# Modulation vectors summed as rows in column quarters, front norms with factors by tokens

## The chip, the cores and the metric

The kernel runs on one core of a Trainium2 chip. The metric is the device time of one execution in microseconds (us), lower is better. Matrix products run on TensorE (PE in the profile; its weight loads are PEld), elementwise work on VectorE (DVE) and ScalarE (ACT), and GpSimd (POOL) and SyncE (SP) mostly issue transfers. All matrix results land in PSUM, eight banks of 128 partitions x 512 values of four bytes; everything else on the chip lies in SBUF.

## The reference

Two transformer-like blocks run one after the other on x, 512 tokens x 1024 features. The first block has two layers (a recurrent mixer, then forgetting attention), each with an MLP of width 4096. The second block has two layers with a linear-attention mixer and a gated MLP, and each of its layers is modulated by six vectors that come from one conditioning vector c:

```python
c_act = jax.nn.silu(c)
for l in range(DEPTH):
    mod = c_act @ ada_w[l] + ada_b[l]              # (1, 6144)
    sh1, sc1, gt1, sh2, sc2, gt2 = [m[:, None, :] for m in jnp.split(mod, 6, axis=-1)]
    h = rms_norm_2(x, norm1_g[l]) * (1 + sc1) + sh1
    p = h @ w_in[l]                                # with v_down beside it in layer 1
    ...
    x = x + gt1 * (mixed @ w_out[l])
    h2 = rms_norm_2(x, norm2_g[l]) * (1 + sc2) + sh2
    gate, up = jnp.split(h2 @ w_gu[l], 2, axis=-1)
    x = x + gt2 * ((jax.nn.silu(gate) * up) @ w_down[l])
```

`rms_norm_2` divides each token by the root of the mean of its 1024 squares plus 1e-6. The change is about `mod` and about the norm in front of `w_in` in both layers.

## The kernel before, in words

x is kept transposed: eight tiles `xT[:, t, :]` of 128 features x 512 tokens. Every weight matrix comes in slabs of 1024 rows x 256 columns. SP fetches a slab into `raw`; ACT rounds it to a high part `whi` (function `hi`, line 848) and DVE makes the low part `wlo = raw - whi` (function `lo`, line 1522). PE then makes three products a tile: high x high, high x low, low x high (lines 2386 to 2388 with the weights stationary, 2445 to 2447 with 128 tokens stationary and 256 weight columns moving). `raw`, `whi` and `wlo` hold two slabs each. A slab costs PE about 11 us, ACT 1.9 us and DVE 2.3 us. The products of small tables in plain four-byte floats show as two records each, every one with its own weight load.

The order of work on each engine is written out by hand. Class `Plan` numbers all products that take a PSUM bank; job j uses bank j mod 8, and PE waits in `start` until job j - 8 was read (`ahead` waits the same way without starting the job). `evacuated` waits until a bank was read, `ready` until it was written. SP's order of slabs is the order in which PE uses them.

**The modulation.** While the first block's MLPs run (`mlp1`, layer 0 for the first vectors, layer 1 for the second), POOL fetches `ada_w` and DVE multiplies and adds it into `ada_acc`, 128 partitions x 6144 columns: the sum over the eight groups of 128 rows, so that only the sum over the partitions is left. `adaln` on PE makes this last sum with 48 products: a block of 128 columns of `ada_acc` stationary, a single column of ones moving, so that each gives one column of 128 values, which is the layout that the rest needs. `adaln` on DVE then adds the bias and makes `gmod`, `shc`. For layer 0 these 48 products stand beside the matmuls of slab "v 0" of the attention layer (`adaln_beside`, line 2605, two products in each of the 24 steps of token blocks 1 to 3, the last one behind them, line 2609); their result is read by DVE after the key heads of slab "k 0". For layer 1 they stand in one piece (line 2484) at the front of the second block.

**The front norm of the second block.** For norms 4 (layer 0) and 6 (layer 1), ACT squares the tiles of x (`norm_squares`, line 878), DVE adds the eight squares (`norm_sums`, lines 1533 and 1536), and PE multiplies by a full matrix of 1/1024 (`mean_square`, line 2467), so that all 128 partitions hold the mean of each of 512 tokens. ACT takes the root of 128 x 512 values (`norm_root`, line 883), DVE the reciprocal (line 1541), and then tile by tile DVE makes value = x * gain * factor (line 1555), ACT the high part (line 890), DVE the low part (line 1562). The first projection, slab "lat", starts with the tile that is ready (`before=normed`), then "gl1" and "k2" follow. Norm 4's squares start only after the last addition to x of the first block (line 1664, add x and the product of the last `down` slab); norm 6's squares already stand between the last additions of layer 0 of the second block.

Steps that the prediction compares with: the head means (line 2477, `head_means`), the token-wise mean of norm 2 (line 2594, four products), the factor rows of norm 0 (line 2537, four products of a broadcast column with the identity), the head factors (line 2797, 32 products with 64 stationary columns and 128 moving), the state inputs (line 2859, 48 products of 64 x 64 x 64) and the pool products (line 3108, four of 512 columns). Line 1666 is DVE's addition to x that reads PSUM with a scale.

## Time and profile before

| | |
|---|---|
| Median of 3 runs | 2925.84 us (2925.13 to 2927.65) |
| Profiled execution, span | 2918.1 us |
| PE busy | 2791.1 us |
| DVE busy | 1587.6 us |
| ACT busy | 988.9 us |
| Bytes read from memory | 277.09 MB |

The span is the time from the first to the last instruction of one profiled execution; the measured time of a run has some us around it. Starts are in us from the start of the span. "PEclk" is the clock that TensorE was granted, 1.00 for 2.4 GHz and 0.50 for 1.2 GHz.

### The profile page before, as it was taken

What the parts mean: (1) busy time and instruction counts of PE and PEld (TensorE: products, weight loads), DVE (VectorE), ACT (ScalarE), POOL (GpSimd) and SP (SyncE); (2) the same over time, 40 slices, a digit from 0 to 9 for tenths busy, and PEclk for the clock granted to TensorE, in tenths of its full rate; (3) what the DMA queues carried; (4) which work ended last, traced back from release to release, by engine and by line L of the source; (5) the groups of instructions that cost most, each with busy time, mean ns of one, the idle gap of its engine ahead of it and who ended that gap; (6) DMA issues with size and microseconds to landing.
All of it is one profiled execution on the core that took longest, in us unless ns stands there. A gap on an engine that the chain in (4) does not pass through costs nothing.

```text
span 2918.1 us, 46007 instructions
## 1 busy us (share of the span) xinstructions
PE 2791.1 (96%) x19577; PEld 2317.3 (79%) x19577; DVE 1587.6 (54%) x2309; ACT 988.9 (34%) x1354; POOL 200.0 (7%) x251
## 2 busy tenths in 40 slices
PE   8899999999999999998899999999988999999998
PEld 7778888897788888777878788887667778888887
DVE  5658777854677777465443553334575443543334
ACT  5643222335532212333333332223533333332223
POOL 4100000000000000010040000000020030000000
PEclk9999999999999999799999999999889999999999
DMA  4334555421145554210022322322220013223222
GB/s 150 101 104 131 180 165 173 156 64 53 52 130 177 176 168 152 66 58 12 3 77 89 99 90 98 101 97 72 72 64 6 24 52 101 95 93 101 95 93 72
DMA packets 238532, 281.98 MB, mean 97 GB/s; under 512 B 7444, under 2 KB 224856, under 8 KB 238344
## 3 DMA queue, kind: packets, MB, share of 16 engines
q1 hardware_dynamic: 225312, 227.07, 24.3%
q0 software_dynamic: 12896, 52.11, 6.0%
q8 instruction: 150, 2.46, 0.4%
q14 instruction: 38, 0.31, 0.0%
q10 hardware_dynamic: 136, 0.03, 0.0%
HBM read 277.09 MB, written 2.10 MB: 96 GB/s over the span
## 4 chain that ended last, share of the span: by engine, by line
PE 91%; DVE 4%; ACT 3%; issue 2%; DMA 0%; ACTq 0%; DVEq 0%; POOL 0%; POOLq 0%
PE psum L2386 25%; PE psum L2388 25%; PE psum L2387 25%; PE psum L2445 1%; PE psum L2446 1%; PE psum L2447 1%; PE psum L2887 1%; PE psum L2902 1%; DVE wlo L1522 1%; PE psum L2484 1%; PE psum L2870 1%; PE psum L2797 1%; ACT whi L848 1%; PE psum L2821 1%; PE psum L2835 1%
## 5 line engine op out<-in xcount | busy, mean ns | idle before, releaser
L2386 PE MATMUL psum<-hh,whi 128*128 128x512 f32 (+1 forms) x2040 | 794.4, 389 | 19.5 <-DVE hl L1562 6.6
L1522 DVE TENSOR_TENSOR wlo<-raw,whi 128x2048 fp32r<-128x2048 f32 x222 | 517.3, 2330 | 514.7 <-ACT whi L848 514.1
L2387 PE MATMUL psum<-hl,whi 128*128 128x512 f32 (+1 forms) x2040 | 787.6, 386 | 0.0
L2388 PE MATMUL psum<-hh,wlo 128*128 128x512 f32 (+1 forms) x2040 | 786.9, 386 | 0.0
L848 ACT ACTIVATE whi<-raw 128x2048 fp32r<-128x2048 f32 x222 | 423.8, 1909 | 550.7 <-PE psum L2388 550.7
L2386 PE MATMUL psum<-mh,whi 128*128 128x512 f32 (+1 forms) x1248 | 486.3, 390 | 3.1 <-issue 2.3
L2387 PE MATMUL psum<-ml,whi 128*128 128x512 f32 (+1 forms) x1248 | 480.1, 385 | 0.0
L2388 PE MATMUL psum<-mh,wlo 128*128 128x512 f32 (+1 forms) x1248 | 479.8, 384 | 0.0
L2386 PEld LDWEIGHTS psum<-hh,whi 128*128 128x128 f32 x2040 | 388.1, 190 | 104.0 <-issue 25.2
L2388 PEld LDWEIGHTS psum<-hh,wlo 128*128 128x128 f32 x2040 | 387.8, 190 | 76.9
L2387 PEld LDWEIGHTS psum<-hl,whi 128*128 128x128 f32 x2040 | 388.0, 190 | 75.9 <-issue 1.0
L2386 PEld LDWEIGHTS psum<-mh,whi 128*128 128x128 f32 x1248 | 235.7, 189 | 48.3 <-issue 4.5
L2388 PEld LDWEIGHTS psum<-mh,wlo 128*128 128x128 f32 x1248 | 235.5, 189 | 46.5
L2387 PEld LDWEIGHTS psum<-ml,whi 128*128 128x128 f32 x1248 | 235.7, 189 | 44.3 <-issue 0.5
L1959 DVE SCALAR_TENSOR_TENSOR rest<-rest,cact 128x192 f32<-128x192 f32 (+1 forms) x448 | 187.7, 419 | 15.8
L1666 DVE SCALAR_TENSOR_TENSOR xT<-psum,mod,xT 128x512 f32<-128x512 f32 x64 | 47.4, 750 | 156.2 <-PE psum L2388 156.2
L1201 ACT ACTIVATE mh<-rest 128x512 fp32r<-128x512 f32 x64 | 40.5, 633 | 253.0 <-DVE rest L1970 253.0
L788 POOL DMA_DIRECT2D rest<-in_ada_w x64 | 56.7, 887 | 920.0 <-DVE rest L1959 618.8
L1664 DVE TENSOR_TENSOR xT<-xT,psum 128x512 f32<-128x512 f32 x80 | 54.5, 684 | 108.7 <-PE psum L2388 108.7
L2333 DVE TENSOR_TENSOR rest<-rest,psum 128x512 f32<-128x512 f32 x40 | 27.5, 688 | 110.8 <-PE psum L2388 110.8
L1480 ACT ACTIVATE mh<-rest 128x512 fp32r<-128x512 f32 x44 | 27.8, 633 | 174.3 <-DVE rest L2333 172.8
L1473 ACT ACTIVATE rest<-psum 128x512 f32<-128x512 f32 x40 | 23.9, 598 | 143.4 <-PE psum L2388 143.2
(451 smaller groups left out, 2848.0 us busy)
## 6 DMA issues: line engine op xcount, KB each, us to landing
rest<-in_ada_w POOLq DMA_DIRECT2D x64, 768.0 KB, 5.3
raw<-in_w_gu SPq DMA_DIRECT2D x44, 1024.0 KB, 5.1
raw<-in_w_in SPq DMA_DIRECT2D x34, 1024.0 KB, 5.2
raw<-in_w_mlp_in SPq DMA_DIRECT2D x32, 1024.0 KB, 5.4
raw<-in_w_mlp_out SPq DMA_DIRECT2D x32, 1024.0 KB, 5.1
raw<-in_w_out SPq DMA_DIRECT2D x16, 1024.0 KB, 5.1
raw<-in_w_down SPq DMA_DIRECT2D x16, 1024.0 KB, 5.1
raw<-in_w_mem_kv SPq DMA_DIRECT2D x8, 1024.0 KB, 5.2
```

Source lines behind the costliest of these rows:

```text
L788: pool.dma_start(ada[:, s % 2, :, :], w[:, :, bass.ds(c * (per * ADA_COLS) + s * ADA_COLS, ADA_COLS)])\
L848: act.activation(whi[:, g % 2, :, :], raw[:, g % 2, :, :], ACT.Copy).then_inc(hi_done, 1)
L1201: act.activation(mh[:, m, :], f_t[:, m % 2, :], ACT.Square).then_inc(hid_hi, 1)
L1522: ins = dve.tensor_tensor(wlo[:, g % 2, :, :], raw[:, g % 2, :, :], f32(whi[:, g % 2, :, :]), ALU.subtract)
L1664: free(dve.tensor_tensor(xT[:, t, :], xT[:, t, :], bank(j), ALU.add), j)
L1666: free(dve.scalar_tensor_tensor(xT[:, t, :], bank(j), gate, xT[:, t, :], ALU.mult, ALU.add), j)
L1959: ins = dve.scalar_tensor_tensor(acc, w, cact[:, k:k + 1], acc, ALU.mult, ALU.add)
L2386: pe.matmul(out, whi_, xhi, start=first, stop=False)
L2387: pe.matmul(out, whi_, xlo, start=False, stop=False)
L2388: return pe.matmul(out, wlo_, xhi, start=False, stop=last)
L2445: pe.matmul(p[:, 0:n], xh[:, k, t], wh, start=(k == 0), stop=False)
L2446: pe.matmul(p[:, 0:n], xl[:, k, t], wh, start=False, stop=False)
```

## The change

- The last sum over partitions of the modulation is made in rows: 12 products with 32 copies of the ones column stationary and 512 columns of `ada_acc` moving. Four of them fill one bank, each its own quarter of 32 partitions (`modulation_rows`). ACT copies each of the three banks to `ada_rows` (`modulation_row`), and PE turns them with 12 products: a block of 128 columns of the rows stationary, four columns of the identity moving (`modulation_turned`), which give columns i, i+4, i+8, i+12 of 16.
- For layer 0 the rows stand behind slab "v 0", the turning products behind slab "k 0". For layer 1 the rows stand ahead of norm 4's mean, four turning products behind that mean, and eight behind the factor rows.
- Norms 4 and 6: the mean is made by tokens (four products of one column), the root and the reciprocal of 128 x 4 values, then four products spread the factors over the partitions into a bank (`factor_rows`), from which DVE's norm reads directly; the bank is given back at the end of the norm.
- Norm 4's squares and sums stand between the last additions of the first block's MLP, as norm 2's do in layer 0.
- ACT takes a root of `rtok` in place early in the last slabs of the second block's MLPs; its values are not used again.

```diff
--- before.py
+++ after.py
@@ -175,8 +175,10 @@
                 self.slab_jobs("v", 1, 1, NT)
                 self.add("ms", 2)
                 self.slab_jobs("v", 1, 0, NT)
+                for r in range(3):
+                    self.add("mr", 0, r)
+                self.slab_jobs("k", 1, 0, NT)
                 self.add("mod", 0)
-                self.slab_jobs("k", 1, 0, NT)
                 for i in range(4):
                     self.add("hn", 1, i)
                 self.slab_jobs("k", 1, 1, NT)
@@ -199,7 +201,10 @@
                         self.add("ms", 2 * l + 1)
                 self.lin("down", (l, c), 4)
         for l in range(2):
+            for r in range(3) if l == 0 else ():
+                self.add("mr", 1, r)
             self.add("ms", 4 + 2 * l)
+            self.add("rb", 4 + 2 * l)
             if l == 0:
                 self.add("mod", 1)
             self.lin("lat", l, 1)
@@ -446,6 +451,7 @@
         f_v = carve(rest, B + 2 * T, 2, T)
         ada = carve(rest, B + 9 * T, 2, KT, ADA_COLS)
         ada_acc = carve(rest, B + 9 * T + 2 * KT * ADA_COLS, N_MOD)
+        ada_rows = [carve(mo, 2 * B, 3, T), carve(rest, B + 9 * T, 3, T)]
 
         mK = [carve(rest, B, 4, MEM), carve(rest, 0, 4, MEM)]
         mV = [carve(rest, B + 2 * T, MT_, T), carve(rest, 2 * T, MT_, T)]
@@ -877,6 +883,18 @@
                         act.wait_ge(S("norm_added"), 7 * (ni - 1) + max(1, t - 3))
                     act.activation(n_sq[:, t % 3, :], xT[:, t, :], ACT.Square).then_inc(S("norm_sq"), 1)
 
+            def modulation_row(l, r):
+
+                j = J["mr", l, r]
+                ready(act, j)
+                free(act.activation(ada_rows[l][:, r, :], bank(j), ACT.Copy), j)
+
+            def root_tokens(ni):
+
+                j = J["ms", ni]
+                ready(act, j)
+                free(act.activation(tk[:, 0, :], bank(j)[:, 0:NT], ACT.Sqrt, bias=epst[:, 0:1]), j)
+
             def norm_root(ni):
                 j = J["ms", ni]
                 ready(act, j)
@@ -1103,6 +1121,8 @@
                         j = J["v", l, 0, b]
                         ready(act, j)
                         free(act.activation(vtok[:, b, 0:SLAB], bank(j)[:, 0:SLAB], ACT.Copy, scale=tk[:, 1, b:b + 1]), j)
+                    for r in range(3):
+                        modulation_row(0, r)
                     hi(slab_of("k", 1))
                     for i in range(4):
                         evacuated(act, J["memk", 1, i // 2, i % 2])
@@ -1192,7 +1212,8 @@
                             hi(g0 + i + 1)
                             if l == 0 and i >= 5:
                                 raw_hi(2, lambda t: V("norm_mix", 8 + t), (2 * i - 10, 2 * i - 9))
-                                norm_squares(2, (2 * i - 10, 2 * i - 9))
+                            if i >= 5:
+                                norm_squares(2 + 2 * l, (2 * i - 10, 2 * i - 9))
                         else:
                             hi(g0 + i + 1, c, 8, J["up", (l, cc), 0, 0] + 2 * i - 1, 16)
                         for b in range(2) if i < 4 else ():
@@ -1205,12 +1226,14 @@
                 mlp1(CHUNKS1 - 1, 0)
                 if l == 0:
                     raw_hi(2, lambda t: V("norm_mix", 8 + t), (6, 7))
-                    norm_squares(2, (6, 7))
+                norm_squares(2 + 2 * l, (6, 7))
 
             for l in range(2):
                 if l == 0:
-                    norm_squares(4)
-                norm_root(4 + 2 * l)
+                    modulation_row(1, 0)
+                root_tokens(4 + 2 * l)
+                for r in (1, 2) if l == 0 else ():
+                    modulation_row(1, r)
                 norm_hi(4 + 2 * l, (l, 0))
 
                 def own_part(name, s, b, c, dst, rows=P):
@@ -1484,6 +1507,8 @@
                         gated(c, i)
                     for i in range(4):
                         hi(plan.slab["fd", (l, c), i] + 1)
+                        if c == 2 and i == 0:
+                            act.activation(rtok[:, 1, :], rtok[:, 1, :], ACT.Sqrt)
                         if c == 2 and i:
                             norm_squares(6 + 2 * l, (2 * i - 2, 2 * i - 1))
                             if l:
@@ -1535,16 +1560,17 @@
                         dve.wait_ge(S("norm_added"), 7 * (ni - 1) + t - 1)
                         dve.tensor_tensor(n_acc, n_acc, n_sq[:, t % 3, :], ALU.add).then_inc(S("norm_added"), 1)
 
-            def norm(ni, gain, shift=None, slab=None):
+            def norm(ni, gain, shift=None):
 
                 evacuated(dve, J["ms", ni])
-                q.mark(dve.reciprocal(n_rstd, n_rs))
-                if slab is not None:
-                    lo(slab)
-                q.settle()
-                norm_apply(ni, gain, shift)
-
-            def norm_apply(ni, gain, shift=None, between=None):
+                dve.reciprocal(tk[:, 1, :], tk[:, 0, :]).then_inc(S("front_factor"), 1)
+                j = J["rb", ni]
+                ready(dve, j)
+                norm_apply(ni, gain, shift, factor=bank(j))
+                dve.wait_ge(S("norm_lo"), 8 * ni + KT)
+                dve.sem_inc(bank_read[j % BANKS], 1)
+
+            def norm_apply(ni, gain, shift=None, between=None, factor=n_rstd):
 
                 for t in range(KT + 1):
                     if between:
@@ -1552,7 +1578,7 @@
                     if t < KT:
                         if 3 <= t:
                             dve.wait_ge(S("norm_lo"), 8 * ni + t - 2)
-                        dve.scalar_tensor_tensor(n_val[:, t % 3, :], xT[:, t, :], gain(t), n_rstd, ALU.mult, ALU.mult)\
+                        dve.scalar_tensor_tensor(n_val[:, t % 3, :], xT[:, t, :], gain(t), factor, ALU.mult, ALU.mult)\
                            .then_inc(S("norm_val"), 1)
                     if t >= 1:
                         s = t - 1
@@ -1979,20 +2005,19 @@
                                 j, t = J["down", (l, cc), i - 4, b], 2 * (i - 4) + b
                                 ready(dve, j, 16 * c)
                                 add_x(j, t)
-                        if l == 0 and cc == CHUNKS1 - 1 and i >= 5:
-                            raw_lo(2, lambda t: V("norm_mix", 8 + t), (2 * i - 10, 2 * i - 9))
-                            norm_sums(2, range(max(1, 2 * i - 10), 2 * i - 8))
+                        if cc == CHUNKS1 - 1 and i >= 5:
+                            if l == 0:
+                                raw_lo(2, lambda t: V("norm_mix", 8 + t), (2 * i - 10, 2 * i - 9))
+                            norm_sums(2 + 2 * l, range(max(1, 2 * i - 10), 2 * i - 8))
                 mlp1(0, 0)
                 for c in loop(dve, CHUNKS1 - 2):
                     mlp1(1, c)
                 mlp1(CHUNKS1 - 1, 0)
                 if l == 0:
                     raw_lo(2, lambda t: V("norm_mix", 8 + t), (6, 7))
-                    norm_sums(2, (6, 7))
+                norm_sums(2 + 2 * l, (6, 7))
 
             for l in range(2):
-                if l == 0:
-                    norm_sums(4)
                 norm(4 + 2 * l, lambda t: gmod[:, 2 * l, t:t + 1], (l, 0))
                 if l == 0:
                     adaln(1)
@@ -2476,12 +2501,39 @@
                     p = start("hn", l, first + i)
                     done(pe.matmul(p[:, 0:n], m[:, :], sq[:, i, 0:n], start=True, stop=True))
 
-            def adaln(l):
-
-                p = start("mod", l)
+            def modulation_rows(l):
+
                 pe.wait_ge(ada_done, 256 * (l + 1) + 16)
-                for n in range(48):
-                    ins = pe.matmul(p[:, n:n + 1], ada_acc[:, n * P:(n + 1) * P], ones[:, 0:1], start=True, stop=True)
+                for r in range(3):
+                    p = start("mr", l, r)
+                    for c in range(4):
+                        ins = pe.matmul(p[32 * c:32 * c + 32, :], ones[:, 0:1].to_broadcast([P, 32]),
+                                        ada_acc[:, (4 * r + c) * T:(4 * r + c + 1) * T], start=True, stop=True)
+                    done(ins)
+
+            def modulation_turned(l, r, p):
+
+                evacuated(pe, J["mr", l, r])
+                for i in range(4):
+                    ins = pe.matmul(p[:, 16 * r + i:16 * r + 16:4], ada_rows[l][:, r, i * P:(i + 1) * P], ident[:, 0:P:32],
+                                    start=True, stop=True)
+                return ins
+
+            def mean_square_tokens(ni):
+
+                pe.wait_ge(S("norm_added"), 7 * ni)
+                p = start("ms", ni)
+                for b in range(NT):
+                    ins = pe.matmul(p[:, b:b + 1], n_acc[:, b * P:(b + 1) * P], mean_all[:, 0:1], start=True, stop=True)
+                done(ins)
+
+            def factor_rows(ni, n):
+
+                pe.wait_ge(S("front_factor"), n)
+                p = start("rb", ni)
+                for b in range(NT):
+                    ins = pe.matmul(p[:, b * P:(b + 1) * P], tk[:, 1, b:b + 1].to_broadcast([P, P]), ident[:, :],
+                                    start=True, stop=True)
                 done(ins)
 
             def query_sums(l, p, src, b, k):
@@ -2594,20 +2646,13 @@
                         ins = pe.matmul(p[:, b:b + 1], n_acc[:, b * P:(b + 1) * P], mean_all[:, 0:1], start=True, stop=True)
                     done(ins)
 
-                    mods = bank(J["mod", 0])
-
-                    def adaln_beside(b, k):
-
-                        if (b, k) == (1, 0):
-                            ahead("mod", 0)
-                            pe.wait_ge(ada_done, 256 + 16)
-                        for n in range(16 * b + 2 * k - 16, 16 * b + 2 * k - 14) if b else ():
-                            ins = pe.matmul(mods[:, n:n + 1], ada_acc[:, n * P:(n + 1) * P], ones[:, 0:1], start=True, stop=True)
-                        return ins if b else None
-                    linear_tokens("v", l, 0, h, NT, beside=adaln_beside)
-                    start("mod", 0)
-                    done(pe.matmul(mods[:, 47:48], ada_acc[:, 47 * P:48 * P], ones[:, 0:1], start=True, stop=True))
+                    linear_tokens("v", l, 0, h, NT)
+                    modulation_rows(0)
                     linear_tokens("k", l, 0, h, NT)
+                    p = start("mod", 0)
+                    for r in range(3):
+                        ins = modulation_turned(0, r, p)
+                    done(ins)
                     head_means(1, 0, mean_128, m_sq1, MEM)
                     linear_tokens("k", l, 1, h, NT)
 
@@ -2755,9 +2800,16 @@
                 mlp1(CHUNKS1 - 1, 0)
 
             for l in range(2):
-                mean_square(4 + 2 * l)
                 if l == 0:
-                    adaln(1)
+                    modulation_rows(1)
+                mean_square_tokens(4 + 2 * l)
+                if l == 0:
+                    modulation_turned(1, 0, ahead("mod", 1))
+                factor_rows(4 + 2 * l, l + 1)
+                if l == 0:
+                    p = start("mod", 1)
+                    modulation_turned(1, 1, p)
+                    done(modulation_turned(1, 2, p))
                 linear("lat", l, 0, h, before=normed(4 + 2 * l))
                 linear("gl1", l, 0, h, blocks=1)
                 if l:
```

## Rows read from the trace of the kernel before

**Rows 1.** Page, part 1: busy time of each engine.

```profile
PE 2791.1 (96%) x19577; PEld 2317.3 (79%) x19577; DVE 1587.6 (54%) x2309; ACT 988.9 (34%) x1354; POOL 200.0 (7%) x251
```

**Rows 2.** PE's waits: us in total, times, longest.

```profile
PE psum L2477 <- DVE mod L1613: 0.9, 1, 0.9
```

**Rows 3.** Chain of waits, 1165 to 1215 us: start, us, what.

```profile
1170.18 0.69 DVE xT L1664
...
1175.56 0.70 DVE rest L1536
1176.30 2.07 PE psum L2467 x2
1178.38 20.27 PE psum L2484 x96
1198.65 0.64 PE psum L2386
```

**Rows 4.** Timeline of DVE, 1158 to 1245 us.

```profile
1179.13 3.35 DVE L1541 RECIPROCAL rest<-rest 128x512 f32<-128x512 f32 x1 [2.88 <-ACT rest L883]
1182.52 1.42 DVE L1555 SCALAR_TENSOR_TENSOR rest<-xT,gmod,rest 128x512 f32<-128x512 f32 x2
1184.06 0.75 DVE L1562 SCALAR_TENSOR_TENSOR hl<-rest,mod,hh 128x512 fp32r<-128x512 f32 x1
...
1192.02 1.63 DVE L1562 SCALAR_TENSOR_TENSOR hl<-rest,mod,hh 128x512 fp32r<-128x512 f32 x2
...
1199.60 2.29 DVE L1522 TENSOR_TENSOR wlo<-raw,whi 128x2048 fp32r<-128x2048 f32 x1
```

**Rows 5.** Stretches: length, PE busy (records), granted clock, DMA share, GB/s.

```profile
1176.30:1198.50 22.20, 22.20 (x98) 0.50 0.00 1
1198.50:1204.50 6.00, 6.00 (x15) 0.50 0.35 99
1204.50:1212.10 7.60, 7.60 (x35) 1.00 0.28 96
```

**Rows 6.** Chain of waits, 2036 to 2052 us.

```profile
2040.67 2.04 PE psum L2467 x2
...
2046.85 0.76 DVE rest L1555
```

**Rows 7.** Stretches of the attention layer, columns as in rows 5.

```profile
597.38:621.07 23.69, 23.69 (x195) 0.94 0.29 90
621.07:632.65 11.58, 11.58 (x99) 1.00 0.32 92
632.65:635.37 2.72, 1.80 (x11) 1.00 0.00 0
```

**Rows 8.** Chain of waits, elsewhere, and line 3108's loads and products.

```profile
593.78 0.80 PE psum L2594 x8
594.60 0.27 ACT tk L1090
...
31.90 1.16 PE psum L2537 x8
...
1268.51 3.64 PE psum L2797 x64
...
1325.35 1.56 PE psum L2859 x96
...
1508.00 3.43 PE psum L3108 x8
...
L3108 PEld LDWEIGHTS psum<-rest x16: 187/190/190, 1507.6 to 2378.4; 128*128 128x128 f32 x16
L3108 PE MATMUL psum<-rest x16: 590/592/592, 1507.8 to 2378.8; 128*128 128x512 f32 x16
```

**Rows 9.** Timelines of DVE and PE around slab xq 0.

```profile
644.35 2.29 DVE L1522 TENSOR_TENSOR wlo<-raw,whi 128x2048 fp32r<-128x2048 f32 x1
...
647.07 0.40 PE L2386 MATMUL psum<-hh,whi 128*128 128x512 f32 x1
```

## What I expect, before the changed kernel was seen

> **What bounds the kernel now.** I read the page first: TensorE is busy for 96% of the 2918.1 us span, VectorE for 54%, ScalarE for 34% [rows 1]. So a microsecond counts if it is one of PE's own, or one in which PE stands. The list of PE's waits names one stand that the change touches, 0.9 us in which the head means (L2477) wait for VectorE's modulation step [rows 2]; the larger ones are seen in the chain of waits at the three places of the change, where PE is missing from the chain.
>
> Front of block two, layer 0 [rows 3]: the last addition to x starts at 1170.18, seven sums of squares follow until 1176.26, the mean product (L2467) takes 2.07 us, the 48 modulation products (96 records) take 20.27 us, and only at 1198.65 does the first projection ("lat") start. In that time VectorE makes the reciprocal (3.35 us) and the whole normed operand: the first low tile is ready at 1184.81, the last at 1193.65 [rows 4]. So the modulation products end last, and behind them stand 14 us of finished norm. They run at half clock, 1.2 GHz [rows 5]: 20.27 / 48 = 0.42 us each. Layer 1 has no such products: mean product at 2040.67, first factor use at 2046.85 [rows 6], and "lat" some 2.4 us later, as the norm's pipeline needs. Attention block, layer 1 [rows 7]: the slab "v 0" takes 23.69 us and "k 0", with as many matmuls of 256 columns and nothing beside them, 11.58 us.
>
> **Part 1, modulation of layer 0 (attention block).** Only the first of v 0's four blocks has nothing beside its matmuls. The mean clock of 0.94 over 23.69 us means 2.8 us at half clock, a loss of 1.4 us that stays. At k 0's pace, 11.58 us for four blocks, the 48 products cost 23.69 - 11.6 - 1.4 = 10.7 us, 0.22 us each at 2.4 GHz. These go. In come 12 products of 512 moving columns, each with 32 stationary columns and its own quarter of the output partitions. No row shows four quarters at full depth, so I bound them. A full-width fp32 product of 512 columns takes 3.43 / 4 = 0.86 us (L3108) [rows 8]. One after another, 12 make 10.3 us; four at a time, 2.6 us. What lies nearest: the head factors (L2797), full depth and 64 columns, 32 products of 128 columns in 3.64 us, are 0.114 us each, where L3108's price scaled to 128 columns is 0.21, so two halves do run together; and L2859, in which a product fills a quarter of the array, makes 48 of 64 columns in 1.56 us, 0.033 each, where the same price scaled gives 0.107: a gain of over three. I take 2.7 us. The 12 turning products have full weights and four moving columns, 0.2 us each as L2594's, 2.4 us. The head means then no longer share a bank with the modulation result: the 0.9 us wait goes [rows 2]; the last third of [rows 7] becomes 1.8 us. Sum: 10.7 + 0.9 - 2.7 - 2.4 = 6.5 us of PE time.
>
> The Trainium skill, "TensorE: Matmul & The Clock Gate", section "Measured speedup vs the span model", gives 2.38 times for three column tiles. Scaled to four that would be about 3.2 times, an estimate from that page, and the sum would lose 0.6 us here and nothing in part 2, where the rows end before the sums. L2797's row has about 1.8 times for two, which agrees with it.
>
> Is this PE time free to be taken? The row copies (three, on ScalarE) come ahead of the high part of "k 1", which was made just after v 0 and still is, some 13 us before k 1. VectorE reads the modulation at the end of k 0, so it now waits for the turning products; queued behind that step are the four key factors and the low part of slab "xq 0", which before ended 0.4 us ahead of PE's first use (646.64 against 647.07) [rows 9]. All four head means now lie on PE between the modulation result and k 1, where before only the last did: the margin becomes about 1 us. Bank numbers shift, but freed banks lie further back than before.
>
> **Part 2, front of block two, layer 0.** Four steps.
> (a) Squares and sums of tiles 0 to 3 move between the last additions. The seven sums after the last addition (ends 1170.87) took 0.77 us each. Four stay behind it, 4 to 7: end 1174.0 instead of 1176.26. Tile 7's square has the time of two sums. The other three go where VectorE waits for PE between two down blocks; it is 54% busy [rows 1] and the last addition itself waits for PE.
> (b) The 12 rows start at 1170.0, as the products that the last addition reads end (the accumulation on VectorE stands ahead of the last two additions), and end at 1172.7: under the sums, at full clock. If they ran in turn, they would end at 1180.2, and everything below would start then.
> (c) Mean by tokens: four products (0.80 us), root 0.27 us, reciprocal of 4 columns 0.2 [rows 8]: 1174.05 to 1175.4. One third of the turning products (0.8) lies in that gap on PE, to 1175.7. Factor rows, four products: 1.16 us with their latency (L2537). VectorE's first product with the factor: 1176.9 instead of 1182.52, where the wide root and the 3.35 us reciprocal stood. It reads the factor from PSUM. No row has that; I charge nothing, and 0.1 us more a step would cost 0.3 us at "lat" and less than the 1.5 us margin below.
> (d) The other eight turning products, 1.6 us at full and 3.4 at half clock, lie under the 2.3 us between the first factor use and the first low tile (1182.52 to 1184.81 [rows 4]). "lat" starts at 1176.9 + 2.4 = 1179.3, at worst 1180.
> Gain: 1198.65 - 1179.4 = 19.2 us. What is late next: the low part of "gl1" is queued on VectorE behind the eight norm tiles and the modulation sums: 11.1 + 1.0 + 2.3 = 14.5 us after the first factor use, 1191.4. "lat" itself took 6.0 us at half clock and 7.6 at full, 13.6 us [rows 5]: it ends at 1192.9. Margin 1.5 us, so this queue caps what a kinder clock could add. The fall of the clock I leave as it is: it was at half for 6.0 us after "lat" began, and PE will again have been lightly used just before. I add 0.3 us here for an earlier return.
>
> **Part 3, layer 1.** Same norm with tokens, no modulation, sums as before. The wide mean product's 2.04 us is more than twice the 0.86 of full clock, so the clock is at half, and I leave it there: mean by tokens 4 x 0.42 = 1.7 us plus 0.2 of latency, root and reciprocal 0.5, factor rows 1.9 to 2.2. First factor use: 2040.67 + 4.5 = 2045.1 instead of 2046.85, gain 1.8 us [rows 6]. At full clock it would be 3.3.
>
> The early Sqrt in the last slabs moves ScalarE's table load forward. Before, the load stood ahead of the root, under VectorE's sums, and the root followed the mean product at once (2.04 us of product, then root and reciprocal in 4.1) [rows 6], so it gains nothing.
>
> **Sum.** 6.5 + 19.2 + 0.3 + 1.8 = 27.8 us. The profiled span of 2918.1 would be 2890.3; the median of the runs, 2925.84, lies 7.7 above the span, and I take this as fixed: 2925.84 - 27.8 = 2898.0 us.
>
> **Rivals.**
> 1. Quarters run two at a time (14%): L2797 is the only full-depth row, and it has two. Rows cost 5.1 us: 2.4 less in part 1; in part 2 they end at 1175.1, 1.1 after the sums. Gain 24.3, 2901.5 us.
> 2. Quarters don't overlap at all (6%): 10.3 us in part 1, a loss of 7.6, and in part 2 the mean starts at 1180.2 instead of 1174.05, a loss of 6.2. Gain 14.0, 2911.8 us. L2797 and L2859 speak against it.
> 3. The other side (2%): each change of quarter drains the array. Then none of the 24 records overlaps with its load or its neighbour: 0.59 us of duration and 0.19 for the load (L3108's), 24 x 0.78 = 18.7 us instead of 2.7, once in part 1 and once from 1170.0 on. Part 1 turns into a loss of 9.5, part 2 keeps 19.5 - 14.7 = 4.8, part 3 1.8: 2.9 us slower, 2928.7 us. The point from which it decides: 0.72 us a record.
> The Trainium skill, "TensorEngine Tiling (Array Packing)", section "Key Properties", says that a change of tiling mode drains TensorE and a change of tile does not. By it only the ends of each group of 12 pay, two per group.
> 4. The gain is kept on PE but the clock answers otherwise (16%): every later stretch at half clock shifts in time and may last longer or shorter; a us more of it costs half a us. In part 2 PE may stay at 2.4 GHz: then the gl1 queue caps it at 1.5 us more. Or the half-clock stretch lasts 3.4 us longer: 1.7 us less, in each of the two fronts. 2894 to 2903 us.
> 5. The change doesn't do what it says (1%): the modulation rows wait for something and lat stays near 1198. Gain about 8, 2918 us.
> The forecast itself has 61%, within 2895 to 2901 us.
>
> **How the numbers follow.** Forecast, rivals 1 and 4 together are 91% and lie within 2893 to 2905; I leave out 2, 3 and 5. For the size of the clock's changes I keep 2893 to 2905.5. The measurement can tell about 0.2%, 5.9 us, from no change. Faster by more: forecast, 1, 2, 4 and 5, 0.97; within: what else could eat 22 us, 0.01; slower: 0.02.
>
> **What would show it.** Right: twelve pairs of row records within 3 us in both places; k 1's start some 31.4 us after v 0's (38.0 before); no wait of L2477; "lat" starting 9.2 us after the last addition of layer 0 began; a factor use 4.5 us after the mean product in layer 1. Wrong: row records 0.43 us or more apart without a partner; a wait of gl1 or xq 0 for their low parts; half clock inside k 0.

## Result: 2896.1 us, and the profile after

The changed kernel takes 2896.09 us in the median of four runs (2891.50 to 2896.93), beside 2925.49 us for the kernel before (2923.75 to 2927.65, four runs): ratio 0.9894, 95% interval 0.9880 to 0.9908; the medians are 29.4 us apart. Run twice more, on the chips of later experiments, it took 2894.07 and 2893.92 us. The predicted 2898.0 us is 1.9 us too slow and its range holds all three. The profiled execution has a span of 2889.9 us, 28.2 us less than before; the sum of the prediction was 27.8 us. Against the kernel before on their own chips the two later medians are 29.6 and 29.4 us lower. Of the experiments below one execution stands out, one of the ten of e9_columns_front, which took 7222.22 us beside 2914 to 2923 us for the other nine (their median is 2919.37 us, that of all ten, in the table below, 2919.94).

The page of the kernel after, part 1 (busy time, share of the span, instructions):

```profile
PE 2775.1 (96%) x19507; PEld 2301.7 (80%) x19507; DVE 1582.7 (55%) x2309; ACT 992.4 (34%) x1362; POOL 200.6 (7%) x251
```

Against [rows 1] TensorE is busy for 16 us less in a span that is 28 us shorter, so it is still the bound; the work of VectorE and ScalarE is the same within 5 us. New line numbers: the three products of a slab are L2411 to L2413, the row products L2510, the turning products L2518, the mean by tokens L2527, the factor rows L2535, the head means L2502, the last sums L1561, the norm's two steps L1581 and L1588, the low parts of slabs L1547.

**Attention block, layer 1** (answers to [rows 7]). The chain of waits of the kernel after, 592 to 645 us (start, us, what):

```profile
597.26 2.21 DVE wlo L1547
...
612.77 2.71 PE psum L2510 x24
...
627.20 2.58 PE psum L2518 x24
629.77 1.83 PE psum L2502 x8
```

The rows stand behind v 0 and the turning products behind k 0, and the head means follow without a wait. "v 0" starts at 599.52 and "k 1" at 631.25: 31.7 us, where before it was 635.37 - 597.38 = 38.0 us. The low part of slab xq 0 is queued behind the modulation step on VectorE (timeline of the kernel after, 636 to 645 us):

```profile
639.66 2.29 DVE L1547 TENSOR_TENSOR wlo<-raw,whi 128x2048 fp32r<-128x2048 f32 x1
```

It ends at 641.95, and the first product of xq 0 starts at 642.95 by TensorE's records: the margin is 1.0 us.

**Front of block two, layer 0** (answers to [rows 3]). The chain of the kernel after, 1164 to 1180 us:

```profile
1166.92 0.04 DVE xT L1690
1166.96 0.57 issue
1167.53 0.70 DVE rest L1561
...
1170.66 1.05 PE psum L2527 x8
1171.71 0.90 PE psum L2518 x8
1172.61 1.00 PE psum L2535 x8
1173.60 2.79 PE psum L2518 x16
1176.39 0.63 PE psum L2411
```

The last addition (L1690) starts at 1166.92. Four sums follow in place of seven, then mean, a third of the turning products, factor rows, the rest of the turning products, and "lat" at 1176.39 (1176.25 by TensorE's own record): 9.4 us behind the last addition, where before it was 1198.65 - 1170.18 = 28.5 us. The rows themselves aren't in the chain. The timeline of TensorE shows them under the sums:

```profile
1166.82 2.78 PE L2510 MATMUL psum<-rest,ones 128*32 128x512 f32 x24
1170.66 1.05 PE L2527 MATMUL psum<-mean_all,rest 128*128 128x1 f32 x8 [1.06 <-DVE rest L1561]
```

**Layer 1** (answers to [rows 6]). The chain of the kernel after:

```profile
2017.09 1.88 PE psum L2527 x8
...
2019.53 2.09 PE psum L2535 x8
...
2021.64 0.76 DVE rest L1581
...
2024.08 0.76 PE psum L2411
```

From mean to the first factor use 4.55 us (before 6.18), from mean to "lat" 6.99 us (before 8.61).

**The account.** Starts after minus starts before: v 0 +2.1 (this arises ahead of every edit; 1.6 of it lie in a stretch at half clock at 33.9 us that the earlier trace lacks), k 1 -4.1, last addition -3.3, lat -22.3, mean of layer 1 -23.6, lat of layer 1 -25.2, end -28.2. So the first stage gives 6.3 us, the second 19.0, the third 1.6, 26.9 in all. Behind lat of layer 1 another 3.0 us go, as the 6.4 us less at half clock there (46.6 for 53.0) would have it. Between lat of layer 0 and the mean of layer 1 it is 1.3 us less although 8.8 us more are at half clock (42.1 for 33.3); why is open.

### The profile page after: what moved, and what is told of

The parts are those of the page before. It is cut to its first block, busy times and chain, and to the rows that moved or that the text cites. A ratio compares the mean times of both kernels' runs of the same rounds, so it can differ in the third digit from the quotient of the medians.

```text
span 2889.9 us, 45888 instructions
## 1 busy us (share of the span) xinstructions
PE 2775.1 (96%) x19507; PEld 2301.7 (80%) x19507; DVE 1582.7 (55%) x2309; ACT 992.4 (34%) x1362; POOL 200.6 (7%) x251
## 3 DMA queue, kind: packets, MB, share of 16 engines
q1 hardware_dynamic: 225312, 227.07, 24.7%
## 4 chain that ended last, share of the span: by engine, by line
PE 91%; DVE 4%; ACT 3%; issue 2%; DMA 0%; ACTq 0%; POOL 0%; DVEq 0%; POOLq 0%
PE psum L2411 25%; PE psum L2413 25%; PE psum L2412 25%; PE psum L2470 1%; PE psum L2939 1%; PE psum L2954 1%; PE psum L2471 1%; PE psum L2472 1%; DVE wlo L1547 1%; ACT whi L854 1%; PE psum L2922 1%; PE psum L2849 1%; PE psum L2873 1%; PE psum L2887 1%; PE psum L2840 1%
## 5 line engine op out<-in xcount | busy, mean ns | idle before, releaser
L2411 PE MATMUL psum<-hh,whi 128*128 128x512 f32 (+1 forms) x2040 | 793.8, 389 | 15.2 <-DVE mo L2125 5.6
L1547 DVE TENSOR_TENSOR wlo<-raw,whi 128x2048 fp32r<-128x2048 f32 x222 | 517.7, 2332 | 507.0 <-ACT whi L854 506.4
L2412 PE MATMUL psum<-hl,whi 128*128 128x512 f32 (+1 forms) x2040 | 786.1, 385 | 0.0
L2413 PE MATMUL psum<-hh,wlo 128*128 128x512 f32 (+1 forms) x2040 | 786.1, 385 | 0.0
L2411 PE MATMUL psum<-mh,whi 128*128 128x512 f32 (+1 forms) x1248 | 486.7, 390 | 3.1 <-issue 2.3
L2412 PE MATMUL psum<-ml,whi 128*128 128x512 f32 (+1 forms) x1248 | 480.2, 385 | 0.0
L2413 PE MATMUL psum<-mh,wlo 128*128 128x512 f32 (+1 forms) x1248 | 479.9, 385 | 0.0
L2411 PEld LDWEIGHTS psum<-hh,whi 128*128 128x128 f32 x2040 | 387.6, 190 | 97.5 <-issue 18.8
L2412 PEld LDWEIGHTS psum<-hl,whi 128*128 128x128 f32 x2040 | 387.7, 190 | 75.9 <-issue 1.0
L2413 PEld LDWEIGHTS psum<-hh,wlo 128*128 128x128 f32 x2040 | 386.9, 190 | 76.5
L2411 PEld LDWEIGHTS psum<-mh,whi 128*128 128x128 f32 x1248 | 235.9, 189 | 48.3 <-issue 4.5
L2413 PEld LDWEIGHTS psum<-mh,wlo 128*128 128x128 f32 x1248 | 235.7, 189 | 46.5
L2412 PEld LDWEIGHTS psum<-ml,whi 128*128 128x128 f32 x1248 | 236.0, 189 | 44.3 <-issue 0.5
L1985 DVE SCALAR_TENSOR_TENSOR rest<-rest,cact 128x192 f32<-128x192 f32 (+1 forms) x448 | 187.7, 419 | 15.8
L1690 DVE TENSOR_TENSOR xT<-xT,psum 128x512 f32<-128x512 f32 x80 | 54.6, 685 | 108.6 <-PE psum L2413 108.6
L1503 ACT ACTIVATE mh<-rest 128x512 fp32r<-128x512 f32 x44 | 27.8, 633 | 174.0 <-DVE rest L2358 172.5
L1496 ACT ACTIVATE rest<-psum 128x512 f32<-128x512 f32 x40 | 23.9, 598 | 143.3 <-PE psum L2413 143.2
```

The source lines that it names most:

```text
L1547: ins = dve.tensor_tensor(wlo[:, g % 2, :, :], raw[:, g % 2, :, :], f32(whi[:, g % 2, :, :]), ALU.subtract)
L1690: free(dve.tensor_tensor(xT[:, t, :], xT[:, t, :], bank(j), ALU.add), j)
L1985: ins = dve.scalar_tensor_tensor(acc, w, cact[:, k:k + 1], acc, ALU.mult, ALU.add)
L2411: pe.matmul(out, whi_, xhi, start=first, stop=False)
L2412: pe.matmul(out, whi_, xlo, start=False, stop=False)
L2413: return pe.matmul(out, wlo_, xhi, start=False, stop=last)
```

## Experiments

All stage times below are read from TensorE's records as above. "Stage A" runs from v 0's start to k 1's (in the runs that move the rows ahead of v 0: from the start of the mean product before it), "stage B" from the first row product (it starts within 0.15 us of the last addition; in before and e9, which have none there, the last addition itself, by the chain) to lat in layer 0, with the part from the mean product to lat in brackets, "stage C" from the mean product to lat in layer 1.

| Run | Stage A | Stage B | Stage C | Median us | Ratio to the kernel before, 95% |
|---|---|---|---|---|---|
| before | 38.0 | 28.5 | 8.6 | | |
| changed | 31.7 | 9.4 (5.6) | 7.0 | 2896.09 | 0.9894 (0.9880 to 0.9908) |
| a1_changed_again | 32.8 | 9.3 (5.4) | 7.0 | 2894.07 | 0.9898 (0.9881 to 0.9916) |
| a2_changed_again | 32.8 | 10.4 (6.5) | 7.0 | 2893.92 | 0.9901 (0.9884 to 0.9917) |
| e1_columns_beside | 38.1 | 9.3 (5.4) | 6.9 | 2906.62 | 0.9943 (0.9923 to 0.9963) |
| e2_wide_norm | 32.7 | 11.6 (7.7) | 8.7 | 2897.02 | 0.9910 (0.9890 to 0.9929) |
| e3_squares_late | 32.7 | 14.8 (8.6) | 7.0 | 2897.39 | 0.9901 (0.9868 to 0.9934) |
| e9_columns_front | 32.9 | 28.5 (24.7) | 7.0 | 2919.94 | 0.9988 (0.9976 to 1.0001) |
| e4_one_quarter | 41.1 | 15.8 (5.4) | 7.0 | 2905.36 | 0.9939 (0.9917 to 0.9962) |
| e5_halves | 37.5 | 10.7 (5.4) | 7.0 | 2899.14 | 0.9911 (0.9892 to 0.9929) |
| e6_rows_first | 32.6 | 10.4 (6.6) | 6.9 | 2891.50 | 0.9892 (0.9875 to 0.9909) |
| e7_front_order | 32.7 | 9.3 (5.4) | 7.0 | 2888.84 | 0.9883 (0.9866 to 0.9899) |
| e8_busy | 32.6 | 9.8 (6.0) | 6.0 | 2890.23 | 0.9887 (0.9870 to 0.9903) |
| e10_busy_both | 32.4 | 9.7 (5.3) | 6.3 | 2887.46 | 0.9872 (0.9856 to 0.9888) |

For e6 to e10 stage A has to be held against 35.5, 36.6 and 36.6 us of the three traces of the changed kernel from the same point.

My theory was the sum of the prediction: products that take 10.7 and 20.3 us of TensorE's own time are replaced by some that take 5.1 us and partly lie under VectorE's work, because four quarters run at once. The rivals were fewer quarters at once, and a gain that comes mostly from the norm or from the clock.

**The changed kernel again, nothing edited**

> The changed kernel once more, on the chip of the next three, so that they are read against it by stage. 2896 us, 0.989 to 0.991 of the kernel before. From v 0's start to k 1's 31.7 us, from the last addition's start in layer 0 to lat 9.3 to 9.5 us, 12 row products in 2.7 us. What lies outside these stages may move by 1 to 3 us with the stretches at half clock, and if it does here, with nothing edited, differences of this size in the other runs are no effect of their edits.

> The changed kernel a third time, as the measure for the next three on their chip. 2894 to 2896 us. Stages as before: mean product to lat 5.4 to 5.6 us in layer 0 and 7.0 us in layer 1, v 0 to k 1 31.7 to 32.8 us, which of the two by how long v 0 runs at half clock.

The spans were 2894.8 and 2892.0 us beside 2889.9. The stages repeat but for the clock. Stretches, columns as in [rows 5], v 0 of the first trace and of a1:

```profile
599.52:612.70 13.18, 13.18 (x96) 0.87 0.52 160
```

```profile
600.59:614.84 14.25, 14.25 (x96) 0.80 0.52 148
```

and, of a2, v 0, the head means, and the last turning products of layer 0:

```profile
599.40:612.36 12.96, 12.96 (x97) 0.89 0.55 163
629.28:632.19 2.91, 2.91 (x10) 0.55 0.02 6
1176.71:1179.99 3.28, 3.28 (x18) 0.50 0.00 0
```

The same 96 records of v 0 cost up to 1.3 us more where the clock comes back later (5.8 us of them at half clock in a1, 3.4 in the first trace, 2.9 in a2), and in a2 it falls again under the head means (2.9 us, against 1.6 in the first trace) and is down under the eight turning products (3.3 us at half clock). With that a2's 6.5 us from the mean product to lat lie outside the 5.4 to 5.6 us that I expected. Over the whole span the three traces have 125, 138 and 126 us at half clock. So a difference of up to 5 us between two spans needs no edit; I judge the other runs by their stages first.

**The modulation of layer 0 put back beside v 0**

```diff
-                    linear_tokens("v", l, 0, h, NT)
-                    modulation_rows(0)
...
+                    linear_tokens("v", l, 0, h, NT, beside=adaln_beside)
+                    start("mod", 0)
+                    done(pe.matmul(mods[:, 47:48], ada_acc[:, 47 * P:48 * P], ones[:, 0:1], start=True, stop=True))
                     linear_tokens("k", l, 0, h, NT)
-                    p = start("mod", 0)
-                    for r in range(3):
-                        ins = modulation_turned(0, r, p)
-                    done(ins)
```

> The changed kernel with part 1 undone: the modulation sums of layer 0 stand again as 48 column products beside slab v 0. My theory is that this place was worth PE time only: removed 10.7 and 0.9 us, added 2.7 and 2.6, so this kernel should be 6.3 us slower than the changed one (about 2902.4 us, 0.992 of the kernel before), with k 1 again 38.0 us after v 0 instead of 31.7 and a 0.9 us wait of the head means. Rival: other engines fill in part of it (the low part of xq 0 came only 0.4 us ahead of PE before), and less than 4 us are lost here.

Stage A is 38.1 us, 5.3 to 6.4 us more than the changed kernel's, and the wait of the head means is back, on VectorE's modulation step. Its timeline of TensorE:

```profile
637.00 0.67 PE L2498 MATMUL psum<-mo,mean 128*128 128x256 f32 x2 [0.92 <-DVE mod L1635]
```

The other stages don't move. The time is 10.5 to 12.7 us longer, more than the stage accounts for. The ratios differ by 0.0045 with a half-width of some 0.0026 (13 us, 6 to 21), so the measurement just includes the stage's 6 us. What the rest is stays open: the profiled execution is e1's fastest, 2901.19 us, and its span is 4.8 to 9.7 us longer than the three of the changed kernel, though it has 109 us at half clock where they have 125 to 138.

**The wide norm put back in both fronts**

```diff
-                root_tokens(4 + 2 * l)
+                norm_root(4 + 2 * l)
...
-                dve.reciprocal(tk[:, 1, :], tk[:, 0, :]).then_inc(S("front_factor"), 1)
...
+                q.step(dve.reciprocal(n_rstd, n_rs))
+                norm_apply(ni, gain, shift)
...
-                mean_square_tokens(4 + 2 * l)
...
-                factor_rows(4 + 2 * l, l + 1)
+                mean_square(4 + 2 * l)
```

> The changed kernel with norms 4 and 6 again wide: one product with the full matrix of 1/1024, root of 128 x 512, reciprocal of 128 x 512. Modulation rows and the early squares stay. My theory: the first factor use lies on the path in both layers. Layer 0: from the end of the sums 2.1 + 0.7 + 3.4 us instead of 3.0, so about 3.2 us later; the turning products are hidden under that. Layer 1: 1.9 us later. Sum 5.1 us slower than the changed kernel, 2901 us. Rival: the turning products of layer 1's modulation fall back to full cost, or the longer stand keeps the clock at half for one more stretch: 7 us or more.

The 12 turning products stand behind the wide mean in one piece here. Chain of e2 from the mean product of layer 0 on (L2487 the wide mean, L1565 the wide reciprocal, L2406 lat):

```profile
1175.34 1.14 PE psum L2487 x2
...
1177.22 3.36 DVE rest L1565
...
1183.05 0.76 PE psum L2406
```

7.7 us from mean to lat in place of 5.4 (a1; the first trace has 5.6 and a2 6.5), and 8.7 in place of 7.0 in layer 1: 2.3 + 1.7 = 4.0 us for factors by tokens, where I expected 5.1. The medians are 1 to 3 us apart, in the same direction and inside their intervals.

**The early squares and sums taken back**

```diff
-                            if i >= 5:
-                                norm_squares(2 + 2 * l, (2 * i - 10, 2 * i - 9))
+                            if l == 0 and i >= 5:
+                                norm_squares(2, (2 * i - 10, 2 * i - 9))
...
+                    norm_squares(4)
                     modulation_row(1, 0)
...
+                if l == 0:
+                    norm_sums(4)
                 norm(4 + 2 * l, lambda t: gmod[:, 2 * l, t:t + 1], (l, 0))
```

> The changed kernel with norm 4's squares and sums again behind the last addition of the first block. My theory: seven sums instead of four behind it, 2.3 us later for the mean product and lat, so 2.3 us slower, 2898.4 us; the modulation rows end 1 us before the sums in the changed kernel and give no cover for the difference. Rival: nothing is lost because PE's rows and the first turning products set the start: under 0.5 us.

The mean starts 6.1 us after the last addition, against 3.7: 2.4 us for three sums, as expected. But TensorE then runs all of the front at half clock. Chain of e3: mean, first turning products, factor rows, the other turning products, lat:

```profile
1173.98 1.87 PE psum L2529 x8
1175.85 1.71 PE psum L2520 x8
1177.56 1.91 PE psum L2537 x8
1179.47 3.21 PE psum L2520 x16
1182.67 0.63 PE psum L2413
```

8.6 us from mean to lat, so stage B is 4.4 to 5.5 us longer than the changed kernel's. That the longer wait for the sums brought the clock down is likely, but one trace doesn't show it. The medians differ by 1.3 to 3.5 us, within an interval of +-0.3%; time alone settles nothing here.

**The modulation of layer 1 put back, as 48 columns behind the factor rows**

```diff
             for l in range(2):
-                if l == 0:
-                    modulation_rows(1)
                 mean_square_tokens(4 + 2 * l)
-                if l == 0:
-                    modulation_turned(1, 0, ahead("mod", 1))
                 factor_rows(4 + 2 * l, l + 1)
                 if l == 0:
-                    p = start("mod", 1)
-                    modulation_turned(1, 1, p)
-                    done(modulation_turned(1, 2, p))
+                    adaln(1)
```

> The changed kernel with layer 1's modulation again as 48 column products in one piece, placed behind the factor rows; norm by tokens and early squares stay. My theory: the products cost 0.42 us each at half clock and PE starts lat only behind them, so the whole gain of the norm is covered by them: they start at about 1173.6 and end at 1194, lat 17.7 us later than in the changed kernel, 2913.8 us. Rival: the products start while the clock is still at 2.4 GHz and keep it there, 0.21 us each: lat at 1184, about 8 us slower than the changed kernel.

Chain of e9 (L2529 the mean, L2503 the columns, L2405 lat):

```profile
1175.19 1.88 PE psum L2529 x8
...
1179.71 20.27 PE psum L2503 x96
1199.98 0.64 PE psum L2405
```

The 96 records take the 20.27 us of [rows 3] again, and 24.7 us lie between mean and lat, 18 to 19 us more than in the changed kernel (expected 17.7). The time gives back nearly all of the gain: 0.9988 (0.9976 to 1.0001). This is the largest term of the sum, shown by itself by the stage. In time e9 is 23.9 to 26.0 us slower than the changed kernel, 5 to 8 us more than the stage accounts for (expected: 2913.8 us), and what these are stays open as in e1. The prices of single edits must not be added either: with the columns behind the factor rows the norm's gain is hidden, and stage B is as long as before.

**All row products into one quarter, and into halves**

```diff
-                        ins = pe.matmul(p[32 * c:32 * c + 32, :], ones[:, 0:1].to_broadcast([P, 32]),
+                        ins = pe.matmul(p[0:32, :], ones[:, 0:1].to_broadcast([P, 32]),
```

> All 12 row products write the same quarter of the output partitions, so none can run beside another. Three quarters of the modulation vectors are left out by this, and the work of every other engine is the same. Theory: the 2.71 us for 24 records come from four quarters at a time. Then each record takes its full 0.43 us here and the 12 products 10.3 us in both places: from v 0 to k 1 31.7 + 7.6 = 39.3 us, in the front of layer 0 the mean waits for the last row (10.3 us after 1166.8 instead of 3.8), 6.4 us more, so lat 15.8 us after the last addition: 14 us slower than the changed kernel, 2910 us, about 0.994. Rival (the moving side alone sets the pace, and any target would do): 2.7 us again and no change of the time. Rival (change of quarter costs something that staying in one saves): below 10.3 us.

For the halves:

```diff
-                        ins = pe.matmul(p[32 * c:32 * c + 32, :], ones[:, 0:1].to_broadcast([P, 32]),
+                        ins = pe.matmul(p[64 * (c % 2):64 * (c % 2) + 64, :], ones[:, 0:1].to_broadcast([P, 64]),
```

> The row products write halves (64 stationary columns) in place of quarters, two products in each half in turn; half of the modulation vectors are overwritten and so left out. Theory: two at a time, 12 x 0.43 = 5.1 to 5.2 us for the 12. From v 0 to k 1 2.4 us more, and in the front of layer 0 the rows end at 1172.0 where the sums end at 1170.7, so 1.3 us more there: 3.7 us slower than the changed kernel, 2900 us, 0.991 to 0.992. This is the price of the first rival of the prediction. Other rival: the pace is set by columns of weights loaded (32 or 64), then under 3 us and no change.

The rows in the front of layer 0, by the chain, first of e4, then of e5:

```profile
1175.81 10.42 PE psum L2510 x24
1186.23 0.98 PE psum L2527 x8
```

```profile
1177.15 5.30 PE psum L2510 x24
1182.45 0.98 PE psum L2527 x8
```

The same 24 records take 10.42, 5.30 and 2.71 us: one, two and four at a time, 0.43 to 0.45 us for each group in turn. In both the rows now end last ahead of the mean product, as the prediction's first two rivals have it. e4 costs 8.3 us in stage A and 6.6 in B, e5 4.7 and 1.5, against the changed kernel on the same chip; the 7.7 and 2.6 of A that are the rows' are as expected, the other 0.6 and 2.1 us lie in v 0, the turning products and the head means, which are partly at half clock (the head means 3.0 and 3.2 us in place of 1.6). In time e4 is 11.3 us slower (expected 14) and e5 5.1 (expected 3.7).

**The rows ahead of v 0**

```diff
-                    linear_tokens("v", l, 0, h, NT)
                     modulation_rows(0)
+                    linear_tokens("v", l, 0, h, NT)
```

The copies of the rows on ScalarE move ahead of those of v 0 with them.

> Layer 0's row products stand ahead of v 0 instead of behind it. There TensorE waits 2.8 us for the low part of v 0 (2.21 us on VectorE and the steps around it), and the rows need no operand of v 0. Theory: the 2.7 us of the rows leave the path altogether, and the engine enters v 0 without having stood still, so that part of the 1.4 us lost at half clock there comes back: from v 0's start to k 1's 31.73 - 2.71 = 29.0 us, less up to 1.4: 2.7 to 4.1 us faster than the changed kernel, 2892 to 2893 us, 0.988. Rival: the rows start at the time of the mean product's end but hold v 0 back, because their records are not done when the low part is there; then the gain is 2.7 less what they overlap, at least 1.5 us. Rival: the copies of the rows on ScalarE now stand ahead of the copies of v 0 and hold a bank, so that v 0 or k 0 waits: up to 1.5 us lost, time as the changed kernel's.

Stretches of e6: rows, v 0, turning products, head means:

```profile
598.16:600.55 2.39, 2.39 (x25) 1.00 0.00 0
601.28:612.80 11.52, 11.52 (x96) 1.00 0.61 182
624.39:626.98 2.59, 2.59 (x26) 1.00 0.00 0
626.98:629.87 2.89, 2.89 (x10) 0.56 0.02 6
```

v 0 runs at 2.4 GHz from its first product and takes 11.5 us in place of 13.0 to 14.3; the rows lie in the wait for its low part. The stage is 32.6 us where the changed kernel has 35.5 to 36.6: 2.9 to 4.0 us (expected 2.7 to 4.1). The median is 2.6 us lower, inside the intervals. The head means are mostly at half clock here, though TensorE had been busy by its records without a pause since v 0's start: what it ran just before them were the turning products, with four moving columns each. This takes back 1.3 us of the gain.

**The order in the front of layer 0** (against e6)

```diff
                 if l == 0:
                     modulation_rows(1)
+                    modulation_turned(1, 0, ahead("mod", 1))
                 mean_square_tokens(4 + 2 * l)
                 if l == 0:
-                    modulation_turned(1, 0, ahead("mod", 1))
+                    modulation_turned(1, 1, bank(J["mod", 1]))
                 factor_rows(4 + 2 * l, l + 1)
                 if l == 0:
                     p = start("mod", 1)
-                    modulation_turned(1, 1, p)
                     done(modulation_turned(1, 2, p))
```

> e6_rows_first, and in the front of layer 0 the first third of the turning products goes ahead of the mean product (into the 1.5 us in which TensorE waits for the sums), the second third between mean product and factor rows, the last behind these: four products behind the factor rows in place of eight. Theory: the products behind the factor rows then take 0.8 us at full clock and 1.6 at half, less than the 2.4 us that the norm needs for its first low tile, so lat never waits for them: mean product to lat 5.4 us, where e6_rows_first had 6.6 and the changed kernel 5.6. Time: e6_rows_first's less 0.2 to 1.2 us, 2890 to 2891.5 us. Rival: with one more row copied on ScalarE ahead of the root, the root is late, 0.5 us more between mean and factor rows: no gain over e6_rows_first.

ScalarE copies the second row ahead of the root with it. From mean to lat 5.4 us, and the chain now runs over the norm (L1582, L1589), not over the turning products, before lat (L2412) starts:

```profile
1174.15 0.76 DVE rest L1582
...
1175.68 0.76 DVE hl L1589
1176.58 0.76 PE psum L2412
```

The median is 5.1 us below the changed kernel's on the same chip; the stages give 3.8 (A) and 1.1 (B). It is also 1.2 us below what I expected, and the intervals of the two ratios overlap. The 5.4 us are not new: a1 has them without the edit. What e7 takes away is the chance of a2's 6.5.

**Dense products without use, in layer 1, then in both fronts** (e8 against e7, e10 against e8)

```diff
+            def busy(n):
...
+                for _ in range(n):
+                    pe.matmul(p, whi[:, g % 2, 0, 0:P], mh[:, 0, :], start=True, stop=True)
...
+                if l:
+                    busy(16)
                 mean_square_tokens(4 + 2 * l)
...
                     done(modulation_turned(1, 2, p))
+                else:
+                    busy(9)
```

> e7_front_order, and in the front of layer 1 TensorE gets 16 dense products without use ahead of the mean product and 9 behind the factor rows, where it otherwise waits. Theory: the clock is at half there because the engine stood still, and the price is 1.6 us on mean product and factor rows (7.0 us from mean product to lat, against 5.4 in layer 0) and up to 2.7 us on the first 5.4 us of lat. If it stays at 2.4 GHz: mean to lat 5.4 us, lat at full clock from its start, of which VectorE's queue (the low part of gl1, some 2.2 us of margin) lets 2.2 us through: 3.8 us less than e7_front_order, 2886.5 to 2887.5 us. Rival (the clock falls whatever these products do): at most no gain. Rival (the products themselves hold the mean up): lost time of 0.2 us each.

```diff
-                if l:
-                    busy(16)
+                busy(l, 16 if l else 3)
...
-                else:
-                    busy(9)
+                busy(l, 9 if l else 7)
```

> e8_busy, and in the front of layer 0 three dense products without use ahead of the mean product and seven behind the last turning products. Theory: the half-clock stretch that begins there 2 to 6 us after the mean product and lasts until 6.1 us into lat is not entered; lat then ends 3 us earlier, and the low part of gl1 is next, with a margin of 1.1 us: 1.1 us less than e8_busy, and a wait of gl1 of about 2 us in TensorE's list. Rival: the seven products need 1.5 us at full clock and 3 at half, so if the clock falls all the same, lat is 0.5 to 1.5 us late: slower than e8_busy by that.

Stretches in layer 1, of e7 (from the mean on) and of e8 (the 16 products; mean and factor rows; the nine; lat):

```profile
2015.09:2025.25 10.16, 7.12 (x24) 0.50 0.01 2
```

```profile
2013.52:2017.52 4.00, 3.79 (x18) 1.00 0.00 0
2017.52:2020.05 2.53, 1.96 (x16) 1.00 0.00 0
2020.05:2023.54 3.49, 3.49 (x12) 0.58 0.00 0
...
2024.00:2034.00 10.00, 10.00 (x45) 1.00 0.00 0
```

The clock stays up for mean and factor rows, then falls all the same, for 3.4 us in place of 10.2. The nine products take 3.5 us, 2.9 of them at half clock, and hold lat back by some 0.8 us (it starts at 2023.54, where factor rows and norm would let it start some 0.8 us sooner: the rows end at 2020.30, and the norm needs 2.4 us more). From the mean to the low-rank products behind the projections it is 39.4 us in e8 and e10 and 41.4 in e7: 2.0 us, where I expected 3.8. In layer 0 of e10 the clock doesn't fall at all, and the cap of the prediction appears. Its stretches, its chain, and TensorE's waits:

```profile
1168.56:1175.54 6.98, 6.98 (x54) 1.00 0.02 6
1175.54:1187.60 12.06, 11.17 (x49) 1.00 0.06 20
```

```profile
1173.11 0.76 DVE rest L1582
...
1183.45 0.76 DVE hl L1589
...
1185.33 2.30 DVE wlo L1548
1187.68 0.50 PE psum L2412
```

```profile
PE psum L2412 <- DVE wlo L1548: 1.0, 1, 1.0
```

From the first factor use to the first product of gl1 it is 14.6 us, all of it VectorE's queue; the wait is 1.0 us, where I expected about 2. From the rows to the low-rank products e10 takes 38.5 us and e7 39.4, so the queue lets 0.9 us through (expected 1.1). In time e8 is 1.4 us above e7, where I expected 3.8 less, and e10 1.4 us below e7, all within the intervals: whether the dense products earn anything over the whole kernel isn't shown. The best median of the study is e10's, 2887.46 us, 6.5 us below the changed kernel on the same chip; the intervals of their ratios just touch (0.9888 and 0.9884).

## Why the prediction was right

**Four quarters at once.** I took 2.7 us for the rows from bounds of 2.6 and 10.3; it is 2.71. L2859's row, whose products fill a quarter of the array each, was a better neighbour than L2797's with two halves. e4 and e5 give the two rivals' prices, 10.42 and 5.30 us (assumed: 10.3 and 5.1). The third rival, a drain at each change of quarter, is out: 24 records in 2.71 us are 0.11 us each, where it decides from 0.72. The estimate of 3.2 times from the Trainium skill, "TensorE: Matmul & The Clock Gate", section "Measured speedup vs the span model", was too low for this kernel: 10.42 / 2.71 is 3.8 times, and two halves give 10.42 / 5.30, 2.0 times.

**Part 1**, 6.5 us: 6.3 in the trace of the changed kernel, 5.2 in the two others. The terms hold (rows 2.7, turning products 2.5 to 2.6 for 2.4, head means without a wait). What I missed is that the clock can fall a second time, under the head means behind the turning products: 1.3 us (a2, e6), or that it comes back later in v 0, 1.1 us (a1). I had written half clock down as something that would prove me wrong inside k 0, and it came just behind it. The margin of xq 0, "about 1 us", is 1.0.

**Part 2**, 19.2 us: 19.0, 19.2 and 18.1 by the three traces. lat 9.2 us after the last addition was forecast; it is 9.4, 9.3 and 10.4. Step (d) held only half: "1.6 us at full and 3.4 at half clock, lie under the 2.3 us" can't be true of 3.4 us. At half clock the eight products end 1.1 us after the norm's first tile (a2, e6), and in the first trace they end last too, by some 0.2 us; e7 mends it. The factor read from PSUM costs VectorE nothing: 0.76 us at L1581 as at L1555. The queue ahead of gl1 was put at 14.5 us (its three terms make 14.4) with a margin of 1.5; e10 measures 14.6, and the margin in the changed kernel is 1.2 (low part ready at 1188.16, first product at 1189.37). The 0.3 us for an earlier return of the clock in lat was a guess: lat takes 13.1, 13.7 and 13.8 us in the three traces and 13.8 before. That the early Sqrt gains nothing was not tested by a run.

**Part 3**, 1.8 us: 1.6. The factor use came 4.55 us after the mean product, forecast 4.5. Not in my sum: the earlier lat leaves less of it at half clock (until 2027.3, 3.2 us into lat, where before it was 5.1 us), 1.0 us more.

**The sum.** 27.8 us by the prediction and 28.2 by the spans agree better than they deserve: the span contains shifts of the clock of several us either way, as a1's 4.9 us longer span of the same kernel shows. The three stages make 26.9 us, the rest of the 28.2 was in no term. Taking the median's 7.7 us above the span as fixed was wrong as well: an execution on record is some 1.6 us above its own span, which leaves 6.1 us by which the profiled execution of the kernel before was faster than the median. That the changed kernel's profiled execution was a fast one too, with a span 6.2 us below its median, is luck; the 1.5 us between 7.7 and 6.2 are most of the 1.9 us by which the forecast was too slow. Rival 4 (the clock answers otherwise) isn't excluded by a total, and it is seen in part: the stretch at half clock that begins in the front of layer 0 is 6.8, 6.8 and 10.2 us long in the three traces. The stages, and e1, e4, e5 and e9, show that the mechanism of the gain is the forecast's.

## What to carry to other kernels

- A sum over partitions that leaves 48 columns in a row of tiny products is better made as rows: wide moving operand, few stationary columns, four column quarters side by side, and a turn at the end. It pays where the products stand on TensorE's path, and most where they stand there at half clock (18 to 19 us in the front, 5 to 6 us beside v 0, here).
- Look at where a small product comes to lie. In a wait of TensorE (ahead of v 0, ahead of the mean) it costs nothing; behind the last thing that the next stage needs it costs its full price, and here that was often the price at half clock.
- To price an edit of a few us, compare the stage, and run the unchanged kernel beside it: its own spans differed by 5 us.

## What the runs showed of the hardware

- Products in different column quarters at full depth overlap almost entirely in four-byte floats: 24 records of 512 columns in 10.42 us (one quarter), 5.30 (halves), 2.71 (quarters). The change from full-width products to quarters and back cost no more than some 0.15 us in all (2.71 against six groups of 0.43).
- The granted clock can fall under an engine that is busy without a pause by its records: e6 has 1.00 during its turning products (busy 2.59 of 2.59 us) and 0.56 during the head means behind them. With dense products in the waits the half-clock stretch of the front was 3.4 us long in place of 10.2 in layer 1 (e8 and e7, one trace each), and in layer 0 (e10, one trace) there was none.
- The places where the clock falls differ between executions of one kernel: v 0 runs at half clock for 3.4, 5.8 and 2.9 us in three traces, and the head means of the third for 2.6 of their 2.9 us.
